# Rotated attention rows stored in reading order, values of four tiles kept in SBUF, query loads ahead of stores

## The chip, the cores and the metric

The kernel runs on one NeuronCore of a Trainium2 chip, in one launch. The time is device microseconds of the whole program. The engines are TensorE (PE, with its weight loads as PEld), VectorE (DVE), ScalarE (ACT), GpSimd (POOL) and SyncE (SP), which here only issues DMAs; 16 DMA engines carry the data. Each engine runs its own list of instructions in order and waits on semaphores.

## The reference

One encoder layer on 2048 tokens of width 1024, fp32. The input is normalised and projected; the columns feed two groups of heads: a sparse attention whose keys an indexer picks, and a gated DeltaNet. Then follow the output projection, an MLP and the last norm.

```python
def sparse_indexer_attention(q, k, v, q_idx, k_idx, w_idx):       # blocks of 128 queries
        rel = jax.nn.relu(jnp.einsum('bqhd,bsd->bqhs', qib, k_idx))
        iscore = jnp.einsum('bqhs,bqh->bqs', rel, wb)             # masked to earlier 64-token chunks
        _, sel = lax.top_k(iscore, topk)                          # 256 keys
        s = jnp.einsum('bqngd,bqknd->bqngk', qg, k_sel) * (A_HEAD_DIM ** -0.5)
        p = jax.nn.softmax(s, axis=-1)
        o = jnp.einsum('bqngk,bqknd->bqngd', p, v_sel)

def reference(x, ...):
        h = rms_norm(x, norm_mix_g)
        (qa, ka, va, qi, ki, wi, qb, kb, vb, zb, bb, ab) = jnp.split(h @ w_in, SPLIT_POINTS, axis=-1)
        qa = rope(qa.reshape(bsz, seq, A_HEADS, A_HEAD_DIM), pos)   # 8 heads of 64
        ka = rope(ka.reshape(bsz, seq, A_KV_HEADS, A_HEAD_DIM), pos)  # 2 heads of 64
        o_a = sparse_indexer_attention(qa, ka, va, qi, ki, wi)
        o_b = gated_deltanet(qb, kb, vb, zb, bb, ab, ...)
        x = x + jnp.concatenate([o_a, o_b], axis=-1) @ w_out
        x = x + jnp.square(jax.nn.relu(rms_norm(x, norm_ffn_g) @ w_ff1)) @ w_ff2
    return rms_norm(x, norm_final_g)
```

Rotating a head of 64 rows needs the head itself and the head with its halves of 32 rows exchanged: x·cos + exchanged(x)·sin.

## The kernel before

All data lies with features on the partitions and tokens on the free axis; a tile is 128 tokens, 16 of them. Matmuls take a high and a low part of each fp32 value, so most operands are split first: ACT rounds the high part, DVE or POOL subtracts it.

There are three stages, each a set of five instruction lists:

1. `norm_and_projection` (0 to about 480 us) normalises the input and projects a part of the columns to `projT` in HBM, one chunk of 128 columns after another.
2. `deltanet_and_selection` (490 to 1463 us) runs the DeltaNet, the indexer's scores and selection, and the projection of the chunks that were left, together. `ROUND` is a hand-written row of 22 slots per round, 18 rounds, 396 slots in all; `ProjectionPlan` and `SelectionPlan` put their steps into these slots. A chain is one chunk times 512 tokens: two halves of matmuls into `p_ps`, evacuation by ACT to `p_out` (`project_out`), and a store by SP (`project_store`). There are 36 chains; 20 of them hold attention queries (chunks C_QA to C_QA+3) or keys (C_KA). For each tile whose scores are wanted, SP loads the indexer's queries in six pieces (`rotated_rows`, lines 496 to 498) and two table rows, POOL rotates them in four steps (`rotation` places load and steps), PE scores, ACT and DVE accumulate. Biases and late scores go to HBM (`biasT`, `scoreT`).
3. `attention_and_mlp` (1463 to 3803 us) runs attention of all 16 tiles in 64 units (four per tile, two heads each) beside output projection and MLP of four token blocks. `OverlapPlan` gives each step a slot; within a slot the list `ORDER` decides. The first 16 units (tiles 0 to 3) run alone, in short slots; then units and dense work (288 loads of weights, `m_raw`, two buffers) share the slots.

What the change and the prediction speak of in stage 3:

- An *item* (`prep_items`) is the k heads (2) or one group of q heads (4) of one tile: 48 in all. `prep_in` loads it as x and exchanged x on 128 partitions, where the two halves of 64 partitions hold the same rows. Items 0 to 11 have five buffers (four in `m_acc`, one in `m_rot`), later ones only `m_rot`; item i waits on `p_done` of the one before in its buffer. DVE multiplies by the cosine (L1992, `by_cosine`), POOL by the sine (L1731), adds (L1738); ACT rounds (L1871); POOL or DVE makes the low part (L1744, L2001). PE's scores (L2122, L2123) need it.
- `table_in` loads the cosine and sine rows of a tile once the tile before has used them (`p_sin`, `p_cos`).
- Values are transposed and split on chip (`m_vsplit`), stored to `valsT` (`values_out`) and read back in pairs of tiles for every unit (`values_back`, `m_vals`, four buffers), 288 loads.
- All of these transfers are issued by SP in its list's order, on one queue.

`rotated_rows` before:

```python
    for base in (0, HD):
        eng.dma_start(a[base:base + HD], src).then_inc(sem_in, 16)
        eng.dma_start(b[base:base + half], src[half:HD]).then_inc(sem_in, 16)
        eng.dma_start(b[base + half:base + HD], src[0:half]).then_inc(sem_in, 16)
```

## Time and profile before

| what | value |
|---|---|
| median of three runs | 3803.68 us (3802.12 to 3806.7) |
| the profiled execution's own time | 3805.14 us |
| its span, first to last instruction | 3803.4 us |
| PE busy | 3389.5 us, 89% |
| DVE, ACT, POOL busy | 55%, 57%, 36% |
| DMA | 306,536 packets, 392.83 MB |
| granted TensorE clock, mean | 0.951 of full speed |

Busy time is time in which an engine executes; issuing a DMA does not count. The profile's 40 slices of 95 us show PE at eight or nine tenths nearly everywhere, with dips at the stages' borders (slices 5, 6 and 16 to 17). A wait is put down to the instruction that released it. Numbers of this profiled execution and of the timed runs differ by 1.5 us.

### The profile page before, as it was taken

The numbers are of one execution on the slowest core, as the hardware profiler recorded it, in microseconds if no ns is written. First come the engines' busy times: TensorE is split into PE (matmuls) and PEld (weight loads), VectorE is DVE, ScalarE is ACT, GpSimd is POOL, SyncE is SP. The second block draws the span as 40 slices with busy tenths as digits, with TensorE's granted clock in tenths as the row PEclk, the third lists the DMA queues.
The fourth block names the chain that finished last, engine by engine and source line by source line (L and its number), as shares of the span: only waits on it lengthen the run. The fifth ranks groups of instructions, "written<-read, shape, count | busy, mean of one in ns | idle before, by whom it ended". The sixth has DMA issues, their size and how long they took to land.

```text
span 3803.4 us, 47244 instructions
## 1 busy us (share of the span) xinstructions
PE 3389.5 (89%) x16866; PEld 2780.1 (73%) x16866; DVE 2073.9 (55%) x3632; ACT 2163.9 (57%) x3717; POOL 1375.3 (36%) x721
## 2 busy tenths in 40 slices
PE   7899967888889994589999889999999999999998
PEld 5678856777777773468777668788777878867886
DVE  4223127787777763636456565757566575433222
ACT  4222127676755552477876859696877944433222
POOL 4111134434254433325344334343323333334442
PEclk9999979999999996699999999999999999999999
DMA  3521151413333243323333333333343333332222
GB/s 115 199 80 70 67 148 50 127 55 80 102 91 86 78 127 104 108 85 112 104 106 117 112 121 107 116 106 123 95 127 120 108 105 101 96 127 84 99 94 78
DMA packets 306536, 392.83 MB, mean 103 GB/s; under 512 B 24688, under 2 KB 231664, under 8 KB 301680
## 3 DMA queue, kind: packets, MB, share of 16 engines
q1 hardware_dynamic: 301552, 358.35, 31.2%
q10 hardware_dynamic: 4752, 31.46, 2.1%
q8 instruction: 136, 2.23, 0.2%
q14 instruction: 96, 0.79, 0.1%
HBM read 323.23 MB, written 66.49 MB: 102 GB/s over the span
## 4 chain that ended last, share of the span: by engine, by line
PE 32%; ACT 13%; DVE 9%; issue 4%; POOL 2%; DMA 1%; SPq 1%; ACTq 0%; DVEq 0%; POOLq 0%
PE m_ps L2059 8%; PE m_ps L2061 8%; PE m_ps L2060 8%; ACT m_junk L1771 5%; PE m_ps L2149 2%; PE m_ps L2137 2%; ACT m_wh L1832 2%; POOL m_wl L1716 1%; ACT m_prob L1859 1%; PE m_ps L2122 1%; ACT m_verdict L1773 1%; PE m_ps L2123 1%; PE m_ps L2102 1%; ACT m_trial L1777 1%; DVE m_rl L1899 1%
## 5 line engine op out<-in xcount | busy, mean ns | idle before, releaser
L1716 POOL TENSOR_TENSOR m_wl<-m_raw,m_wh 128x1024 fp32r<-128x1024 f32 x288 | 717.0, 2490 | 1360.2 <-ACT m_wh L1832 1360.2
L2059 PE MATMUL m_ps<-m_ah,m_wh 128*128 128x512 f32 x1280 | 528.0, 413 | 27.5 <-DVE m_al L1916 16.4
L2061 PE MATMUL m_ps<-m_ah,m_wl 128*128 128x512 f32 x1280 | 506.6, 396 | 0.0
L2060 PE MATMUL m_ps<-m_al,m_wh 128*128 128x512 f32 x1280 | 506.0, 395 | 0.0
L2059 PE MATMUL m_ps<-m_th,m_wh 128*128 128x512 f32 x1024 | 426.4, 416 | 26.0 <-DVE m_tl L1901 11.2
L2061 PE MATMUL m_ps<-m_th,m_wl 128*128 128x512 f32 x1024 | 406.2, 397 | 0.0
L2060 PE MATMUL m_ps<-m_tl,m_wh 128*128 128x512 f32 x1024 | 405.7, 396 | 0.0
L1771 ACT ACTIVATE m_junk<-m_sc,m_trial 128x1152 int8<-128x1152 f32 (+7 forms) x248 | 401.4, 1619 | 4.4 <-DVE m_sc L2019 3.3
L1832 ACT ACTIVATE m_wh<-m_raw 128x1024 fp32r<-128x1024 f32 x288 | 302.8, 1051 | 155.0 <-PE m_ps L2061 139.7
L2059 PEld LDWEIGHTS m_ps<-m_ah,m_wh 128*128 128x128 f32 x1280 | 244.3, 191 | 84.7 <-DVE m_al L1916 19.9
L1177 DVE SCALAR_TENSOR_TENSOR i_score<-i_relu,i_w,i_score 128x512 f32<-128x512 f32 (+3 forms) x266 | 276.5, 1048 | 52.0 <-ACT i_relu L1035 38.6
L1899 DVE TENSOR_TENSOR m_rl<-m_rl 128x512 f32<-128x512 f32 x128 | 106.5, 832 | 361.6 <-ACT m_th L1791 361.2
L1848 ACT ACTIVATE m_phi<-m_ps 128x512 fp32r<-128x512 f32 (+1 forms) x288 | 164.5, 571 | 243.4 <-PE m_ps L2137 238.9
L1894 DVE TENSOR_TENSOR m_acc<-m_acc,m_ps 128x512 f32<-128x512 f32 x256 | 175.0, 685 | 210.0 <-PE m_ps L2061 208.3
L2061 PEld LDWEIGHTS m_ps<-m_ah,m_wl 128*128 128x128 f32 x1280 | 244.2, 191 | 53.7
L1979 DVE TENSOR_TENSOR m_plo<-m_ps,m_phi 128x512 fp32r<-128x512 f32 (+1 forms) x288 | 189.4, 659 | 166.2 <-ACT m_phi L1848 164.9
L2060 PEld LDWEIGHTS m_ps<-m_al,m_wh 128*128 128x128 f32 x1280 | 245.0, 191 | 46.4 <-issue 3.1
L2059 PEld LDWEIGHTS m_ps<-m_th,m_wh 128*128 128x128 f32 x1024 | 196.7, 192 | 72.8 <-DVE m_tl L1901 12.9
L1035 ACT ACTIVATE i_relu<-i_ps 128x512 f32<-128x512 f32 (+3 forms) x304 | 156.2, 545 | 140.8 <-PE i_ps L833 101.4
L1959 DVE CUSTOM_DVE_ANT_0 m_prob<-m_ps,m_bias 128x512 f32<-128x512 f32 (+3 forms) x320 | 192.5, 606 | 73.7 <-PE m_ps L2123 71.5
L2061 PEld LDWEIGHTS m_ps<-m_th,m_wl 128*128 128x128 f32 x1024 | 195.9, 191 | 43.4
L2060 PEld LDWEIGHTS m_ps<-m_tl,m_wh 128*128 128x128 f32 x1024 | 196.8, 192 | 41.1 <-issue 5.0
(313 smaller groups left out, 7510.9 us busy)
## 6 DMA issues: line engine op xcount, KB each, us to landing
m_raw<-w_units SPq DMA_DIRECT2D x288, 512.0 KB, 3.6
m_vals<-valsT SPq DMA_DIRECT2D x256, 128.0 KB, 3.7
p_raw<-w_proj SPq DMA_DIRECT2D x72, 256.0 KB, 4.4
projT<-work ACTq DMA_DIRECT2D x12, 1024.0 KB, 3.8
g_qkvz<-projT SPq DMA_DIRECT2D x16, 768.0 KB, 6.2
wraw<-w_proj SPq DMA_DIRECT2D x21, 512.0 KB, 3.5
projT<-p_out SPq DMA_DIRECT2D x36, 256.0 KB, 3.1
work<-xT SPq DMA_DIRECT2D x8, 1024.0 KB, 5.5
```

The costliest lines, as they stand in the source:

```text
L1035: nc.scalar.activation(relu[:, c % RELUS, 0:w], ips[:, c % 2, 0:w], ACT.Relu).then_inc(relu_done, 1)
L1177: nc.vector.scalar_tensor_tensor(out=to, in0=relu[:, c % RELUS, 0:w], scalar=w_idx[:, j, h:h + 1], in1=to, op0=ALU.mult, op1=ALU.add).then ...
L1716: nc.gpsimd.tensor_tensor(wl[:, n % 3, :], raw[:, n % 2, :], wh[:, n % 3, :].bitcast(fp32), ALU.subtract).then_inc(w_lo, 1)
L1771: turns.do(nc.scalar.activation(junk[:, 0:N], sc[:, 0:N], ACT.Sign, scale=-1.0, bias=trial[:, :].bitcast(fp32), accum_out=balance[:, :]))
L1832: nc.scalar.activation(wh[:, n % 3, :], raw[:, n % 2, :], ACT.Copy).then_inc(w_hi, 1)
L1848: nc.scalar.activation(p_hi[:, m % 2, 0:w], t_bank(r)[:, 0:w], ACT.Copy).then_inc(hi_done, 1)
L1894: nc.vector.tensor_tensor(acc[:, k, :], acc[:, k, :], f_bank(c), ALU.add).then_inc(y_added, 1)
L1959: nc.vector.tensor_tensor_reduce(out=prob[:, u % 2, h, 512 * p:512 * p + w], in0=s_bank(n)[:, 0:w], in1=bias[:, 512 * p:512 * p + w], scal ...
L1979: nc.vector.tensor_tensor(p_lo[:, m % 2, 0:w], t_bank(r)[:, 0:w], p_hi[:, m % 2, 0:w].bitcast(fp32), ALU.subtract).then_inc(lo_done, 1)
L2059: nc.tensor.matmul(dst, hi, rh, start=first, stop=False)
L2060: nc.tensor.matmul(dst, hi, r_low, start=False, stop=False)
L2061: return nc.tensor.matmul(dst, lo, rh, start=False, stop=last)
```

## The change

Five edits, in two stages.

**Layout in HBM.** Two new tensors, `rowsQ` [2 groups, 64 rows, 16 tiles, 2 (x, exchanged x), 4 heads x 128] and `rowsK` [64, 16, 2, 2 heads x 128]. `project_store` writes the 20 chains of queries and keys there, x and exchanged x, with three transfers for each of its two heads, in place of one transfer to `projT`. `p_out` has two buffers, with a semaphore each.

**Loading.** `prep_in` loads an item with one transfer: per row one run of 2 x 4 x 128 (or 2 x 2 x 128) floats, and the 64 rows go to both halves of the partitions by a leading dimension of two with step 0 in the source.

**Values.** `m_vsplit` has five places: tiles 0 to 3 keep theirs, later tiles share the fifth. `product` of tiles 0 to 3 reads them there; `values_back` runs only from tile 4 on, with its buffers counted from unit 16.

**Query loads of the indexer.** `rotation` puts the load first in its slot, ahead of the bias or score store, and the four steps of POOL begin six slots later in place of four.

```diff
     def rotation(self, j, slot):
         slot = max(slot, self.queries_at(j) + 1)
-        self.put("sp", slot, ("load", j))
-        slot += 4
+        self.parts.setdefault(("sp", slot), []).insert(0, ("load", j))
+        slot += 6
...
+        p_stored = [sem(f"p_stored{u}") for u in range(2)]
+        rotated = lambda n: C_QA <= rest.chains[n][1] <= C_KA
+        stores = lambda u, n: 16 * sum(6 if rotated(m) else 1 for m in range(u, n + 1, 2))
...
             def project_store(n):
                 b, c = rest.chains[n]
                 sp.wait_ge(p_left, n + 1)
-                sp.dma_start(projT[c, :, 512 * b:512 * (b + 1)], p_out[:, :]).then_inc(p_stored, 16)
+                if not rotated(n):
+                    sp.dma_start(projT[c, :, 512 * b:512 * (b + 1)], p_out[:, n % 2, :]).then_inc(p_stored[n % 2], 16)
+                    return
+                for h in range(2):
+                    own = p_out[HD * h:HD * (h + 1), n % 2, :].rearrange("p (t s) -> p t s", s=P)
+                    to = rowsK if c == C_KA else rowsQ[(c - C_QA) // 2]
+                    at = (h if c == C_KA else 2 * ((c - C_QA) % 2) + h) * P
+                    own_to = lambda half: to[:, 4 * b:4 * (b + 1), half, at:at + P]
+                    half = HD // 2
+                    sp.dma_start(own_to(0), own).then_inc(p_stored[n % 2], 16)
+                    sp.dma_start(own_to(1)[0:half], own[half:HD]).then_inc(p_stored[n % 2], 16)
+                    sp.dma_start(own_to(1)[half:HD], own[0:half]).then_inc(p_stored[n % 2], 16)
...
             def project_out(n):
                 act.wait_ge(p_done, 2 * (n + 1))
-                if n:
-                    act.wait_ge(p_stored, 16 * n)
+                if n >= 2:
+                    act.wait_ge(p_stored[n % 2], stores(n % 2, n - 2))
...
-                ready = kept[t] if i == self.turns(t) - 1 else self.first
-                self.put("sp", max(ready + 1, product_slot[m - 4] + 1 if m >= 4 else self.first), "values_back", u, i)
+                ready = kept[t] if i == self.turns(t) - 1 else kept[t - 1] if t else self.first
+                if t >= 4:
+                    self.put("sp", max(ready + 1, product_slot[m - 4] + 1), "values_back", u, i)
...
-        v_split = sb("m_vsplit", [P, KV_HEADS, 2 * HD], f32r)
+        v_split = sb("m_vsplit", [P, 5, KV_HEADS, 2 * HD], f32r)
...
             def prep_in(i, before):
-                row, n = (C_KA * P, KV_HEADS) if what == "k" else (C_QA * P + what * G * HD, G)
-                rotated_rows(sp, prep_rows(i, 0), prep_rows(i, 1),
-                             rows[row:row + n * HD, tokens(t)].rearrange("(h r) s -> r h s", r=HD), rot_in[prep_slot(i)])
+                src = (rowsK if what == "k" else rowsQ[what])[:, t].rearrange("r f n -> r (f n)")
+                sp.dma_start(prep_flat(i), src.unsqueeze(0).to_broadcast([2, HD, src.shape[1]])).then_inc(rot_in[prep_slot(i)], 16)
...
             def product(u, i):
-                pe.wait_ge(v_back[m % 4], 16 * (m // 4 + 1))
+                if t < 4:
+                    pe.wait_ge(v_done, t + 1)
+                    v_of = lambda c: v_split[:, c, u % 4 // 2, :]
+                else:
+                    k = back_at(u, i)
+                    pe.wait_ge(v_back[k % 4], 16 * (k // 4 + 1))
+                    v_of = lambda c: vals[:, k % 4, c - 2 * i, :]
...
             def values_back(u, i):
-                if m >= 4:
+                k = back_at(u, i)
+                if k >= 4:
                     sp.wait_ge(pv_done, m - 3)
-                if end == t + 1:
-                    sp.wait_ge(v_kept, 16 * (t + 1))
+                sp.wait_ge(v_kept, 16 * (t + 1 if end == t + 1 else t))
```

How it moves instructions is shown at three places. First SP's list in the opening of stage 3, around the first weights (`m_raw`). Before, the last pieces of item 4 (`m_rot`), the weights, and the pieces of item 5:

```order
L496 DMA m_rot<-projT 64x4x128
L497 DMA m_rot<-projT 32x4x128
L498 DMA m_rot<-projT 32x4x128
L496 DMA m_rot<-projT 64x4x128
L497 DMA m_rot<-projT 32x4x128
L498 DMA m_rot<-projT 32x4x128
L1626 DMA m_raw<-w_units 128x1024 x4
L496 DMA m_acc<-projT 64x4x128
L497 DMA m_acc<-projT 32x4x128
L498 DMA m_acc<-projT 32x4x128
```

After, items 0 to 4 and the weights:

```order
L1662 DMA m_table<-cosT 128x128
L1662 DMA m_table<-sinT 128x128
L1655 DMA m_acc<-rowsK 128x1x512
L1667 DMA m_vraw<-projT 128x128
L1655 DMA m_acc<-rowsQ 128x1x1024 x2
L1655 DMA m_acc<-rowsK 128x1x512
L1655 DMA m_rot<-rowsQ 128x1x1024
L1648 DMA m_raw<-w_units 128x1024 x4
L1655 DMA m_acc<-rowsQ 128x1x1024
```

Six pieces of an item have become one row, so that five rows stand where thirty did, in the same order of items; the line of the issue is 1655 now.

Second, SP's list in stage 2 where the bias of a tile is stored (`biasT`) and the next indexer queries are loaded (`i_rot`). Before:

```order
L678 DMA biasT<-i_ties 128x384
L683 DMA p_raw<-w_proj 128x512
L689 DMA projT<-p_out 128x512
L678 DMA biasT<-i_ties 128x512
L496 DMA i_rot<-projT 64x8x128
L497 DMA i_rot<-projT 32x8x128
L498 DMA i_rot<-projT 32x8x128
```

After:

```order
L702 DMA rowsQ<-p_out 64x4x128
L703 DMA rowsQ<-p_out 32x4x128
L704 DMA rowsQ<-p_out 32x4x128
L702 DMA rowsQ<-p_out 64x4x128
L703 DMA rowsQ<-p_out 32x4x128
L704 DMA rowsQ<-p_out 32x4x128
L682 DMA biasT<-i_ties 128x384
L496 DMA i_rot<-projT 64x8x128
L497 DMA i_rot<-projT 32x8x128
```

The load of the queries now stands between the two bias stores, not behind both, and the store of a chain of queries (`projT<-p_out` before) has become six rows to `rowsQ`.

Third, POOL's list in the second round of stage 2: the first tile's rotation (`i_rot`, `i_qlo`) beside DeltaNet steps (`g_Y`, `g_G`) and low weights (`p_lo`). Before:

```order
L748 TENSOR_TENSOR i_rot<-i_rot,i_table 128x1024
L750 TENSOR_TENSOR i_rot<-i_rot,i_table 128x1024
L753 TENSOR_TENSOR i_rot<-i_rot 128x1024
L787 TENSOR_TENSOR g_Y<-s_ident,g_Ds 128x512
L756 TENSOR_TENSOR i_qlo<-i_rot,i_qhi 128x1024
L801 TENSOR_TENSOR p_lo<-p_raw,p_hi 128x512
```

After:

```order
L764 TENSOR_TENSOR i_rot<-i_rot,i_table 128x1024
L803 TENSOR_TENSOR g_Y<-s_ident,g_Ds 128x512
L766 TENSOR_TENSOR i_rot<-i_rot,i_table 128x1024
L769 TENSOR_TENSOR i_rot<-i_rot 128x1024
L772 TENSOR_TENSOR i_qlo<-i_rot,i_qhi 128x1024
L817 TENSOR_TENSOR p_lo<-p_raw,p_hi 128x512
```

The steps of the rotation begin later, so that `g_Y` of the DeltaNet comes between its first and its second step.

## Rows read from the trace of the kernel before

**Rows 1.** Busy us by stage: window, length, PE, PEld, DVE, ACT, POOL, PEclk, DMA, GB/s
```profile
490.00:1463.00 973.00, 830.77 (x5010) 697.13 (x5010) 691.32 (x1208) 592.94 (x1201) 416.04 (x262) 0.95 0.35 95
1463.00:1611.00 148.00, 58.97 (x273) 47.61 (x274) 70.13 (x223) 53.43 (x137) 52.86 (x49) 0.62 0.41 119
1611.00:3335.00 1724.00, 1620.46 (x7867) 1325.84 (x7866) 1028.09 (x1903) 1252.68 (x2060) 633.84 (x301) 0.97 0.35 109
3335.00:3803.00 468.00, 440.35 (x1863) 351.51 (x1862) 140.42 (x186) 140.14 (x183) 185.71 (x74) 0.97 0.28 96
```

**Rows 2.** PE's waits, 1463 to 1700 us: us in total, times, longest
```profile
PE m_ps L2122 <- POOL m_qlo L1744: 28.1, 2, 26.0
PE m_ps L2158 <- DVE m_mixed L1943: 26.4, 15, 4.4
```

**Rows 3.** PE's waits for DMA, 1620 to 3340 us (the only one)
```profile
PE m_ps L2149 <- DMA m_vals<-valsT: 0.4, 1, 0.4
```

**Rows 4.** Timeline of SP, opening: start, us, engine, line, operation, what, count
```profile
1465.41 0.58 SPq L496 DMA_DIRECT2D m_acc<-projT  x1
...
1482.78 0.43 SPq L498 DMA_DIRECT2D m_rot<-projT  x1
1483.26 9.99 SPq L1626 DMA_DIRECT2D m_raw<-w_units  x4
```

**Rows 5.** Timeline of ACT, POOL and PE, opening; idle time before in brackets
```profile
1487.12 1.06 ACT L1832 ACTIVATE m_wh<-m_raw 128x1024 fp32r<-128x1024 f32 x1 [14.54 <-DMA m_raw<-w_units]
1488.25 4.64 POOL L1716 TENSOR_TENSOR m_wl<-m_raw,m_wh 128x1024 fp32r<-128x1024 f32 x2 [16.13 <-ACT m_wh L1832]
...
1497.50 0.48 PE L2122 MATMUL m_ps<-m_keys,m_qhi 128*128 128x128 f32 x1 [26.00 <-POOL m_qlo L1744]
```

**Rows 6.** Timelines of POOL, then DVE: rows that stand for tables and query rows
```profile
1507.43 0.97 POOL L1731 TENSOR_TENSOR m_acc<-m_acc,m_table 128x256 f32<-128x256 f32 x1 [6.96 <-DMA m_table<-sinT]
...
1526.54 0.97 POOL L1731 TENSOR_TENSOR m_acc<-m_acc,m_table 128x256 f32<-128x256 f32 x1 [6.06 <-DMA m_table<-sinT]
...
1543.85 0.73 POOL L1731 TENSOR_TENSOR m_rot<-m_rot,m_table 128x256 f32<-128x256 f32 x1 [2.63 <-DMA m_table<-sinT]
...
1580.70 0.69 DVE L1992 TENSOR_TENSOR m_rot<-m_rot,m_table 128x512 f32<-128x512 f32 x1 [5.98 <-DMA m_rot<-projT]
...
1595.88 0.68 DVE L1992 TENSOR_TENSOR m_rot<-m_rot,m_table 128x512 f32<-128x512 f32 x1
```

**Rows 7.** DMA, 3400 to 3700 us: packets; queue with MB, share; issues, KB, landing
```profile
DMA packets 7645, 27.98 MB, mean 93 GB/s; under 512 B 848, under 2 KB 848, under 8 KB 7632
...
q1 hardware_dynamic: 7632, 27.79, 27.2%
...
m_raw<-w_units SPq DMA_DIRECT2D x53, 512.0 KB, 3.4
```

**Rows 8.** Window of the first stage with the highest DMA share; columns as in rows 1
```profile
120.00:140.00 20.00, 12.37 (x46) 10.09 (x47) 1.69 (x1) 6.17 (x6) 7.07 (x3) 0.74 0.95 358
```

**Rows 9.** DMA issues, whole span: KB each, median us from issue to landing
```profile
m_raw<-w_units SPq DMA_DIRECT2D x288, 512.0 KB, 3.6
...
m_rot<-projT SPq DMA_DIRECT2D x126, 64.0 KB, 2.9
...
m_table<-cosT SPq DMA_DIRECT2D x16, 64.0 KB, 2.0
```

**Rows 10.** Timelines of SP and ACT: one weights load and its split
```profile
2503.91 0.35 SPq L1626 DMA_DIRECT2D m_raw<-w_units  x1
...
2516.55 1.05 ACT L1832 ACTIVATE m_wh<-m_raw 128x1024 fp32r<-128x1024 f32 x1
```

**Rows 11.** SP's longest wait, 490 to 1463 us
```profile
SPq L689 <- ACT p_out L1111: 348.6, 32, 31.4
```

**Rows 12.** Waits of POOL and of PE, 490 to 1463 us
```profile
POOL i_rot L748 <- DMA i_table<-sinT: 63.8, 8, 15.7
...
PE p_ps L963 <- POOL p_lo L801: 16.6, 5, 4.0
```

More of the change, by code:

```diff
@@ L521, in deltanet_and_selection @@
         q_hi, q_lo = sb("i_qhi", [P, 2, IDX_HEADS, P], f32r), sb("i_qlo", [P, 2, IDX_HEADS, P], f32r)
-        p_out = sb("p_out", [P, 512])
+        p_out = sb("p_out", [P, 2, 512])
         ones = sb("g_ones", [P, P])
@@ L583, in deltanet_and_selection @@
         w_in = [sem(f"p_w_in{u}") for u in range(rest.RAW)]
-        p_high, p_low, p_done, p_left, p_stored = map(sem, " p_high p_low p_done p_left p_stored".split())
+        p_high, p_low, p_done, p_left = map(sem, " p_high p_low p_done p_left".split())
+        p_stored = [sem(f"p_stored{u}") for u in range(2)]
+        rotated = lambda n: C_QA <= rest.chains[n][1] <= C_KA
+        stores = lambda u, n: 16 * sum(6 if rotated(m) else 1 for m in range(u, n + 1, 2))
         dve_s, act_s, pool_s, pe_s = sem("g_dve"), sem("g_act"), sem("g_pool"), sem("g_pe")
@@ L662, in selection @@
                         if stored_chains:
-                            sp.wait_ge(p_stored, 16 * (max(stored_chains) + 1))
+                            for u in range(2):
+                                sp.wait_ge(p_stored[u], stores(u, max(stored_chains)))
                         rotated_rows(sp, rot[:, 0], rot[:, 1], rows[C_QI * P:C_QI * P + IDX_HEADS * HD, tokens(j)]
@@ L727, in _ @@
                 sp.wait_ge(kept[u], 16 * len([z for z in plan.late_piece.values() if z % 4 == u]))
-            sp.wait_ge(p_stored, 16 * len(rest.chains))
+            for u in range(2):
+                sp.wait_ge(p_stored[u], stores(u, len(rest.chains) - 1))
         @block.gpsimd
@@ L1105, in project_out @@
                 act.wait_ge(p_done, 2 * (n + 1))
-                if n:
-                    act.wait_ge(p_stored, 16 * n)
-                else:
+                if n >= 2:
+                    act.wait_ge(p_stored[n % 2], stores(n % 2, n - 2))
+                elif n == 0:
                     for u in range(2):
                         act.wait_ge(z_stored[u], 16 * ((N_PROJECTED + 1 - u) // 2))
-                nc.scalar.activation(p_out[:, :], pps[:, :], ACT.Copy).then_inc(p_left, 1)
+                nc.scalar.activation(p_out[:, n % 2, :], pps[:, :], ACT.Copy).then_inc(p_left, 1)
             run_turns(selection, ("act", {"high": project_high, "evac": project_out, "block": project_block}), front, back)
@@ L1611, in attention_and_mlp, with prep_flat @@
         heads_of = lambda i: 2 if plan.prep_items[i][1] == "k" else 4
+        def prep_flat(i):
+            r = acc[:, 2 * prep_slot(i):2 * prep_slot(i) + 2, :] if prep_slot(i) < 4 else rot[:, :, :]
+            return r.rearrange("p f n -> p (f n)")[:, 0:2 * heads_of(i) * P]
         def prep_rows(i, half):
-            r = acc[:, 2 * prep_slot(i):2 * prep_slot(i) + 2, :] if prep_slot(i) < 4 else rot[:, :, :]
-            return r[:, half, 0:heads_of(i) * P].rearrange("p (h s) -> p h s", s=P)
+            return prep_flat(i)[:, half * heads_of(i) * P:(half + 1) * heads_of(i) * P].rearrange("p (h s) -> p h s", s=P)
+        v_own = lambda t: v_split[:, min(t, 4), :, :]
+        back_at = lambda u, i: plan.turn[u, i] - plan.turn[16, 0]
         last_turn = lambda u: plan.turn[u, plan.turns(u // 4) - 1]
@@ L1654, in values_back @@
                 end = min(2 * i + 2, t + 1)
-                if m >= 4:
+                k = back_at(u, i)
+                if k >= 4:
                     sp.wait_ge(pv_done, m - 3)
-                if end == t + 1:
-                    sp.wait_ge(v_kept, 16 * (t + 1))
-                sp.dma_start(vals[:, m % 4, 0:end - 2 * i, :].bitcast(fp32),
-                             valsT[2 * i:end, :, g * P:(g + 1) * P].rearrange("c p d -> p c d")).then_inc(v_back[m % 4], 16)
+                sp.wait_ge(v_kept, 16 * (t + 1 if end == t + 1 else t))
+                sp.dma_start(vals[:, k % 4, 0:end - 2 * i, :].bitcast(fp32),
+                             valsT[2 * i:end, :, g * P:(g + 1) * P].rearrange("c p d -> p c d")).then_inc(v_back[k % 4], 16)
             def score_load(n):
@@ L1836, in values_hi @@
                 act.wait_ge(ring_done, r + 1)
-                if t:
+                if t > 4:
                     act.wait_ge(v_kept, 16 * t)
-                nc.scalar.activation(v_split[:, :, 0:HD], t_bank(r)[:, 0:P].rearrange("p (g d) -> p g d", d=HD),
+                nc.scalar.activation(v_own(t)[:, :, 0:HD], t_bank(r)[:, 0:P].rearrange("p (g d) -> p g d", d=HD),
                                      ACT.Copy).then_inc(v_high, 1)
@@ L2148, in product @@
                         at = 2 * P * (c - 2 * i)
-                        last = nc.tensor.matmul(o, vals[:, m % 4, c - 2 * i, :], part[:, m % 2, at:at + 2 * P],
+                        last = nc.tensor.matmul(o, v_of(c), part[:, m % 2, at:at + 2 * P],
                                                 start=(c == 0 and part is p_hi), stop=(c == t and part is p_lo))
@@ L2164, in _, with program @@
                     does[what](*x)
-def program(nc, S, a, projT, biasT, scoreT, valsT, mixT, xhT, xlT, outT):
+def program(nc, S, a, projT, rowsQ, rowsK, biasT, scoreT, valsT, mixT, xhT, xlT, outT):
     topk = min(TOPK_MAX, S // 4)
@@ L2252 @@
     xhT, xlT = [nc.dram_tensor(n, (S // 512, P, KC, 512), fp32, kind="Internal").ap() for n in ("xhT", "xlT")]
+    rowsQ = nc.dram_tensor("rowsQ", (2, HD, S // P, 2, 4 * P), fp32, kind="Internal").ap()
+    rowsK = nc.dram_tensor("rowsK", (HD, S // P, 2, KV_HEADS * P), fp32, kind="Internal").ap()
     mixT = nc.dram_tensor("mixT", (KC, P, S), fp32, kind="Internal").ap()
     outT = nc.dram_tensor(_OUT, (KC, P, S), fp32, kind="ExternalOutput").ap()
-    program(nc, S, a, projT, biasT, scoreT, valsT, mixT, xhT, xlT, outT)
+    program(nc, S, a, projT, rowsQ, rowsK, biasT, scoreT, valsT, mixT, xhT, xlT, outT)
     r = run_bass_kernel_spmd(nc, [arrays], core_ids=[0])
```

18 lines of the change are left out of this document (9 added, 9 removed).

## The prediction

> **What bounds the kernel now.** I read the busy times by stage first. TensorE (PE) is busy for 94% of the long stretch from 1611 to 3335 us and for 94% of the last one, and 85% of the time from 490 to 1463; in the 148 us from 1463 to 1611 it is busy for 59 us [rows 1]. So time is bought by PE work everywhere but in that gap, the opening of the attention stage, where only query and key rows are rotated and the first 16 small units run. The granted clock there is 0.62 in the mean, so it stands much of the time at the lower of its two levels (1.2 GHz), against 0.95 to 0.97 elsewhere; PE has little to do before and in it. PE's waits in 1463 to 1700 come next: 28.1 us for the low part of the queries (one wait of 26.0) and 26.4 on DVE's normalising [rows 2]. In 1620 to 3340 PE waits for a transfer for 0.4 us in all [rows 3]: nothing that the change does to DMA can buy time there, it can only cost.
>
> **The opening as it is.** SP issues two table loads and then five items (k and two q of tile 0, k and q of tile 1) as 30 pieces, 1465.41 to 1483.21, before it reaches the weights [rows 4]. The weights land at 1487.1, ACT and POOL split two units, POOL rotates, and PE's first score is at 1497.50 [rows 5]. After that the next tile's cosine table is late behind other issues: POOL stands 7.0 us until 1507.4, 6.1 until 1526.5 and 2.6 until 1543.9, DVE with it at the first two, and DVE 6.0 until 1580.7 for the q rows of tile 4 [rows 6].
>
> **What the edit takes away there.** An item is one issue: 30 issues become 5 at 0.43 to 0.58 us, which saves about 15 us in front of the weights. In the first four tiles the 24 reads of values go, and SP waits less for `pv_done`. Were every load to land as quickly as loads do now, this is worth: first score 13 us earlier (15 of issue, less 2 because 2.5 MB at 358 GB/s [rows 8] then take 7 us with the weights at their end); the table of tile 1 needs only `p_sin` and `p_cos`, so 5.5 of the 7.0 us go; 4 of the 6.1 at the second (beyond that DVE has other work); 5 of the 6.0 at 1580.7; 2.9 at the mix loads, where six pieces sit between the third and fourth [rows 4, 6]. Sum 13 + 5.5 + 4 + 5 + 2.9 = 30.4 us.
>
> **What the new load costs: the deciding term.** No row of the trace shows a load like the new one. Its source access is [2 copies, step 0] x [64 rows] x [run], its destination 128 rows. All loads and stores before have 16, 32, 64 or 128 rows outermost on both sides. How work is dealt to the 16 DMA engines can be read where weights run alone: 53 loads of 512 KB make 7,632 packets, 144 each, and 848 of them are small, 16 for each load [rows 7]. That is 128 rows of 4 KB, eight to each engine, and a closing packet on each of 16. So a transfer is dealt out by its outermost rows. The new one has two outermost. Dealt as now, it lands as the weights do, in 3.6 us [rows 9]; dealt in two, each engine gets 64 rows. The trace gives 27.79 MB in 27.2% of 16 x 300 us, 21.3 GB/s per engine [rows 7], and 358 GB/s at a share of 0.95, 23.6 GB/s [rows 8]: 256 KB per engine takes 11.1 to 12.3 us for a q item, half as much for a k item, plus about 2 us to land (the small table loads: 2.0 us [rows 9]). The bounds of this term are thus 3.6 and 14.3 us per q item. The nearest row by size is the lower; by shape there is none, and I take the upper, because the dealing that rows 7 show leaves no other place to cut. The chances below carry the doubt.
>
> The Trainium skill ("DMA: Bandwidth & Descriptors", Rules for kernel authors) says it outright: a leading zero-stride broadcast of c copies confines the whole DMA to at most c engines. No run here shows it yet; by that rule the time is the slow one.
>
> **The walk through the opening, two engines.** All loads are on SP's one queue, so whatever follows has its share on those two engines behind them. With 12.3 and 6.1 us (in brackets with 11.1 and 5.6):
> 1. Ahead of the weights stand 3 q and 2 k items: 49 us (44.5). The weights' own share is 1.5, landing 2: 1465.4 + 49 + 1.5 + 2 = 1518, against 1487.1: +31 (+26). The splits, rotation and first score follow as in [rows 5]: PE starts at 1528 in place of 1497.5.
> 2. The next q and k items are issued after the fourth weights load and at the first score; table 1 stands behind both and lands at 1546.7, where the shifted row would want 1538.5: +8.2 (+6.4).
> 3. Three items (q, q, k) are freed only by the rows after table 1 and stand ahead of table 2: +16.3 (+13.3).
> 4. Two q items stand ahead of table 3, where there was slack of 2.6 us on POOL alone: +11.8 (+9.4).
> 5. The q items of tile 4: the first behind 2 MB of x, +6.5 (+4.6); the second, which DVE wants at 1595.9 [rows 6] and which is issued when the first is done, +6.8 (+5.6); a k item ahead of the fourth mix load: +2.4 (+1.5).
> Sum 83 (67); I take the middle, **+75 us**. The 30 us of savings are not subtracted: SP's issues are no longer what ends any of these waits, the landings are. The clock is not a term of its own; the late start keeps PE at the lower level for longer in a stretch that waits on data anyway.
>
> **The long stretch.** Eleven more tiles load two q and a k item each, 20 us or more apart, and cos and sin wait for them far less soon. But weights land behind them. A weights load is used late: issued at 2503.91, split by ACT at 2516.55 [rows 10], so 12.6 less 3.6 leaves 9 us of cover. A q item issued up to 7.6 us earlier (the spacing of weights: 1724 us over some 225 units) delays it by 4.7 to 12.3 us: in some half of 22 cases ACT stands 0 to 3 us. PE takes over a part: +6 us, between 0 and 25. The values' reads have about three turns of lead and go with it.
>
> **The middle stage (490 to 1463).** 20 of 36 stores of the projection become six pieces: 5 x 0.53 us more each, 53 us of SP's time. SP waits 348.6 us there just for ACT to leave a chain, so the weights behind it have cover [rows 11]; without it each store would cost 2.7 us. The query loads now stand ahead of the bias and score stores, and their rotation is two slots later. POOL stood 63.8 us for these loads, PE 16.6 us for the low weights that POOL makes behind them [rows 12]: a gain of up to 12. Against it, scores start two slots later and end at slot 385 in place of 381 of 396: some 5 scores of 0.8 us PE move to the end, and order shifts of up to 10 us either way. I take -3 (-12 to +10). The double `p_out` frees 2.7 us of ACT at most.
>
> Sum: 75 + 6 - 3 = +78 on the span of 3803.4, 3881. The profiled run itself took 3805.1, 1.5 over the median of 3803.7; on the median the forecast is **3882 us**, with 3840 to 3920 as its own range (67 - 12 - 15 for packets somewhat quicker; 83 + 25 + 10).
>
> **Rivals.**
> - *Loads are dealt to 16 engines* (faster). The price is then 3.6 us in place of 14.3 and the opening gains 30.4 us; with 3 from the middle stage 3770. It decides if a q item lands in less than about 5 us. For it: the 126 pieces of 64 KB land 2.9 us after issue in the median [rows 9], the bytes are the same and the runs are longer. Against: these have no copy dimension.
> - *Two engines, but other transfers do not queue behind* (slower, less). Then the weights are early and the first score waits for q alone: 1465.4 + 6.1 + 12.3 + 2, and 4.6 of rotation and rounding give 1490. Only the items' own stream of 31 us for each tile binds: the last q of tile 3 lands near 1591 where it is wanted at 1556, +33, and tile 4's add 12: 3850.
> - *The price is hidden or offset* (no change): it takes twelve items in 110 us; two engines need 100 to 112 us for them before any gap, so hiding needs loads that never wait for a free slot, and they do (`p_done`).
> - *The edit does not do what it says*: rows would be read in the wrong order or six pieces remain; the order of the program shows one.
>
> **Chances.** Two engines with the queue behind them 0.62; the same with free lanes 0.14; sixteen engines 0.18; the rest 0.06. A measurement of this kernel tells 0.2% (7.6 us) from no change. Faster 0.17, same 0.05, slower 0.78. The range that leaves out less than 2 in 10 must reach to the fast rival: 3766 to 3925.
>
> **What would show it.** For the two-engine price: q items that land 12 us or more after issue with a DMA share of about 0.13 while SP sits in waits; the first weights near 1518, first score near 1528 (if the middle stage ends at the same time); stands of POOL and DVE put down to the sine table and to `m_rot`, of 16 and 12 us; an opening of some 220 us in place of 148. Against it: q items at 4 us, weights at about 1474 and the first score at 1484. The stores' price shows as SP's waits for `p_left` shrinking by about 50 us with no new wait of ACT on the projection's weights; the long stretch's as ACT waits on `m_raw`. If PE's busy time in the long stretch falls under 92%, the +6 was too small. I am wrong if the first score comes earlier than 1497.

## The result, and the profile after

The changed kernel takes 3875.99 us (median; 3869.3 to 3881.1), the kernel before on the same chip 3802.9: ratio 1.0188, 95% interval 1.0175 to 1.0201. It is slower, 6 us under the forecast of 3882. The profiled execution's span is 3870.8 us, 67.4 more than before.

Three instants divide it. They are read from PE's timeline: the last matmul of the middle stage (L848 before, L864 after), the first score, and the first dense matmul.

| profile | middle stage ends | first score | first dense matmul | span | timed ratio |
|---|---|---|---|---|---|
| before | 1456.6 | 1497.5 | 1611.4 | 3803.4 | |
| after | 1440.2 | 1506.2 | 1666.7 | 3870.8 | 1.0188 |
| difference of the stretch | -16.4 | +25.1 | +46.6 | +12.1 | |

So the opening costs 71.8 us more, the rest of the stage 12.1, and the middle stage gives 16.4. By stage, as in [rows 1], with the borders where this kernel has them (window, length, busy us of PE, PEld, DVE, ACT, POOL, then PEclk, DMA share, GB/s):

```profile
490.00:1441.00 951.00, 818.95 (x5010) 693.78 (x5010) 683.58 (x1208) 590.49 (x1199) 412.30 (x261) 0.96 0.40 101
1441.00:1667.00 226.00, 62.11 (x277) 50.80 (x277) 71.44 (x225) 55.60 (x140) 54.50 (x50) 0.58 0.21 69
1667.00:3391.00 1724.00, 1608.96 (x7811) 1315.71 (x7811) 1025.92 (x1897) 1247.08 (x2049) 631.54 (x299) 0.97 0.35 108
```

PE does the same work in the opening (62 us) in 226 us, and the DMA engines, at a share of 0.21, are less busy there than the 0.41 of [rows 1]. In the next 1724 us PE is busy 11.5 us less than before: that is the +12.

SP's timeline of the opening, which answers to [rows 4] (start, us, line, what):

```profile
1448.96 0.62 SPq L1655 DMA_DIRECT2D m_acc<-rowsK  x1
...
1450.10 4.18 SPq L1655 DMA_DIRECT2D m_acc<-rowsQ  x2
1454.32 9.94 SPq L1655 DMA_DIRECT2D m_acc<-rowsK  x1
1464.30 9.97 SPq L1655 DMA_DIRECT2D m_rot<-rowsQ  x1
```

The instructions that wait for these items, on DVE, ACT and PE (as in [rows 5]; idle time before in brackets):

```profile
1457.50 1.00 DVE L2013 TENSOR_TENSOR m_acc<-m_acc,m_table 128x256 f32<-128x256 f32 x1 [16.40 <-DMA m_acc<-rowsK]
1467.78 0.69 DVE L2013 TENSOR_TENSOR m_acc<-m_acc,m_table 128x512 f32<-128x512 f32 x1 [9.29 <-DMA m_acc<-rowsQ]
...
1495.81 1.06 ACT L1853 ACTIVATE m_wh<-m_raw 128x1024 fp32r<-128x1024 f32 x1 [35.99 <-DMA m_raw<-w_units]
...
1506.20 0.47 PE L2143 MATMUL m_ps<-m_keys,m_qhi 128*128 128x128 f32 x1 [48.01 <-POOL m_qlo L1765]
```

The q item, 512 KB, lands 10.3 us after the k item ahead of it. From 1467.8, a q, a k and a q item more (10.3 + 5.1 + 10.3, k taken as half) and some 2 us for the weights make 1495.5: they are there at 1495.81. The window in which only items run shows how many engines carry them:

```profile
1455.00:1475.00 20.00, 0.45 (x1) 0.18 (x1) 2.11 (x3) 0.42 (x1) 1.45 (x2) 0.50 0.13 51
```

A share of 0.13 of 16 is two engines, with 51 GB/s. Of PE's clock this row says that it stands at the lower level (0.50, 1.2 GHz), where PE had been idle for the 16.6 us before 1457.7. The stands of POOL (its idle time in front of an instruction) that answer to [rows 6], first three for tables, then for the q rows of tile 4:

```profile
1521.94 0.97 POOL L1752 TENSOR_TENSOR m_acc<-m_acc,m_table 128x256 f32<-128x256 f32 x1 [12.77 <-DMA m_table<-sinT]
...
1554.34 0.97 POOL L1752 TENSOR_TENSOR m_acc<-m_acc,m_table 128x256 f32<-128x256 f32 x1 [19.37 <-DMA m_table<-sinT]
...
1581.32 0.73 POOL L1752 TENSOR_TENSOR m_rot<-m_rot,m_table 128x256 f32<-128x256 f32 x1 [12.30 <-DMA m_table<-sinT]
...
1626.60 1.77 POOL L1752 TENSOR_TENSOR m_rot<-m_rot,m_table 128x512 f32<-128x512 f32 x1 [18.53 <-DMA m_rot<-rowsQ]
```

Two views of waits, for the rest. First 490 to 1463 us (as in [rows 11, 12]), then all after 1667 us (as in [rows 3]):

```profile
SPq L702 <- ACT p_out L1127: 192.7, 19, 20.5
...
SPq L694 <- ACT p_out L1127: 118.4, 14, 17.1
...
POOL i_rot L764 <- DMA i_table<-sinT: 17.0, 6, 5.8
...
PE p_ps L979 <- POOL p_lo L817: 4.1, 2, 2.8
```

```profile
PE m_ps L2176 <- DMA m_vals<-valsT: 9.4, 5, 4.3
ACT m_wh L1853 <- DMA m_raw<-w_units: 7.7, 4, 3.6
```

### The profile page after: what moved, and what is told of

Same layout as the page of the kernel before. It is cut to its first block, busy times and chain, and to the rows that moved or that the text cites. A ratio compares the mean times of both kernels' runs of the same rounds, so it can differ in the third digit from the quotient of the medians.

```text
span 3870.8 us, 47278 instructions
## 1 busy us (share of the span) xinstructions
PE 3382.9 (87%) x16866; PEld 2781.4 (72%) x16866; DVE 2064.7 (53%) x3632; ACT 2163.1 (56%) x3717; POOL 1373.5 (35%) x721
## 3 DMA queue, kind: packets, MB, share of 16 engines
q1 hardware_dynamic: 276240, 360.96, 31.2%
## 4 chain that ended last, share of the span: by engine, by line
PE 30%; ACT 12%; DVE 8%; DMA 4%; issue 4%; POOL 2%; SPq 1%; ACTq 0%; DVEq 0%; POOLq 0%
PE m_ps L2080 8%; PE m_ps L2082 8%; PE m_ps L2081 8%; ACT m_junk L1792 5%; PE m_ps L2176 2%; PE m_ps L2158 2%; ACT m_wh L1853 2%; POOL m_wl L1737 1%; ACT m_prob L1880 1%; PE m_ps L2143 1%; PE m_ps L2144 1%; ACT m_verdict L1794 1%; ACT m_trial L1798 1%; PE m_ps L2123 1%; DMA out_dram<-m_tmp 1%
## 5 line engine op out<-in xcount | busy, mean ns | idle before, releaser
L2080 PE MATMUL m_ps<-m_ah,m_wh 128*128 128x512 f32 x1280 | 529.1, 413 | 27.5 <-DVE m_al L1937 16.6
L1193 DVE SCALAR_TENSOR_TENSOR i_score<-i_relu,i_w,i_score 128x512 f32<-128x512 f32 (+3 forms) x266 | 252.7, 957 | 49.5 <-ACT i_relu L1051 35.0
L1051 ACT ACTIVATE i_relu<-i_ps 128x512 f32<-128x512 f32 (+3 forms) x304 | 156.0, 546 | 166.9 <-PE i_ps L849 132.3
```

The source lines that it names most:

```text
L1051: nc.scalar.activation(relu[:, c % RELUS, 0:w], ips[:, c % 2, 0:w], ACT.Relu).then_inc(relu_done, 1)
L1193: nc.vector.scalar_tensor_tensor(out=to, in0=relu[:, c % RELUS, 0:w], scalar=w_idx[:, j, h:h + 1], in1=to, op0=ALU.mult, op1=ALU.add).then ...
L2080: nc.tensor.matmul(dst, hi, rh, start=first, stop=False)
```

## The experiments

My theory, A: the transfer is dealt to the DMA engines by its outermost dimension, here of two entries, and everything behind it on the queue waits. Rivals: the new layout in HBM, or the copying itself, is slow. A second question is what the other edits are worth. All ratios below are against the kernel before on the same chip.

**e1: an item in two transfers.**

```diff
-                sp.dma_start(prep_flat(i), src.unsqueeze(0).to_broadcast([2, HD, src.shape[1]])).then_inc(rot_in[prep_slot(i)], 16)
+                for base in (0, HD):
+                    sp.dma_start(prep_flat(i)[base:base + HD], src).then_inc(rot_in[prep_slot(i)], 16)
```

> The changed kernel, but an item is loaded by two transfers, one for each half of 64 partitions, so that 64 rows are outermost in each; everything else stays. Theory A (a transfer is dealt to the DMA engines by its outermost dimension, and two outermost entries are what costs): an item lands in about 4 us, the weights about 15 us after the first item's issue plus 7, first score some 27 us after the middle stage's end instead of 66. The opening's +72 goes and the 30.4 us worked out for the saved issues come; with the 16.5 us that the middle stage gained in the profile of the changed kernel: 3803.4 - 16.5 - 30.4 = 3757, between 3750 and 3775. Theory B (the cost lies in the new layout in HBM or in its reads, whoever carries them): no change, 3876 as the changed kernel, over 3850.

Measured: 3765.4 us, ratio 0.9898 (0.9884 to 0.9913), span 3762.9. It is faster than both kernels. SP, ACT and PE, and a window with items only:

```profile
1449.84 1.14 SPq L1656 DMA_DIRECT2D m_acc<-rowsK  x2
...
1456.60 12.73 SPq L1648 DMA_DIRECT2D m_raw<-w_units  x4
```
```profile
1463.20 1.06 ACT L1854 ACTIVATE m_wh<-m_raw 128x1024 fp32r<-128x1024 f32 x1 [7.56 <-DMA m_raw<-w_units]
...
1473.60 0.48 PE L2144 MATMUL m_ps<-m_keys,m_qhi 128*128 128x128 f32 x1 [19.55 <-POOL m_qlo L1766]
```
```profile
1452.00:1460.00 8.00, 0.45 (x1) 0.18 (x1) 2.11 (x3) 0.42 (x1) 1.45 (x2) 0.50 0.96 239
```

The same bytes from the same place, with 64 rows outermost: the share goes from 0.13 to 0.96, and 110 us of the kernel's time go with it. Layout and stores are the same, so theory B falls. The first score is 32.6 us after the middle stage's end, 8.3 nearer than in the kernel before, but later than the 27 expected. The items' ten issues take 6.8 us (1449.84 to 1456.60) where thirty took 17.9, 11.1 less and not 15; and the first weights are there 6.6 us after their issue, behind the items, where it was 3.9 [rows 4, 5]. (The expectation of e9 below puts this first score at 1474.8: that is the fifth score matmul.) The opening (end of the middle stage to first dense matmul) is 132.3 us, against 154.8 before and 226.6 after; the rest of the stage, 2189.5, has lost its +12.

**e2 and e5: no copy.** The lower half of the partitions gets other rows, by a step of the source that is not 0; which heads or tokens these are is wrong, nothing else changes. e2 takes the other group of query heads (for k the neighbouring tile), e5 the neighbouring tile for both:

```diff
-                src = (rowsK if what == "k" else rowsQ[what])[:, t].rearrange("r f n -> r (f n)")
+                src = (rowsK if what == "k" else rowsQ[what])[:, t // 2 * 2:t // 2 * 2 + 2].rearrange("r a f n -> a r (f n)")
```

> The changed kernel with one transfer for an item, two outermost entries as there, but the second entry is other data (the other group of query heads, or the neighbouring tile's keys) instead of the same rows again, so the lower half of the partitions gets wrong rows. Theory A (it is the two outermost entries): time as the changed kernel, 3876 within 8; a q item every 10.3 us. Theory B (it is the copy, that is step 0 or reading the same addresses twice): the time falls to about 3757 as with 16 engines.

> As e2_two_sources, whose q items read rows 0 to 127 of one block at a constant distance, so that two and 64 could be joined to 128 rows. Here the second entry is always the neighbouring tile (4 KB or 2 KB away, while the rows are 64 or 32 KB apart), for q and for k, so that two entries stay outermost; half of the rows are of the wrong tile. Nothing is copied. Theory A (two outermost entries that can't be joined with the rows): as the changed kernel, 3876 within 8, q items 10 us apart, DMA share 0.13 while they run. Theory B (a copy with step 0, or reading the same addresses twice, is what costs): about 3765, as e1_two_loads.

e2 gave 3787.9 us, 0.9957 (0.9942 to 0.9971), which fits neither theory as I had written them. The fault was in the design: group 1 of `rowsQ` begins just where row 64 of group 0 would stand, so the q items' access is 128 rows at one distance, not two times 64. Its trace bears this out: two q items are issued in 0.91 us, the seven in `m_acc` land in 6.9 us in the median, and in the 3 us in which the first two run all 16 engines are busy.

```profile
1448.25 0.91 SPq L1658 DMA_DIRECT2D m_acc<-rowsQ  x2
```
```profile
m_acc<-rowsQ SPq DMA_DIRECT2D x7, 512.0 KB, 6.9
```
```profile
1450.00:1453.00 3.00, 0.00 (x0) 0.00 (x0) 0.00 (x0) 0.00 (x0) 0.00 (x0) 0.50 1.00 301
```

Only the k items keep two outermost entries there. e5 closes that gap: 3871.5 us, 1.0182 (1.0164 to 1.0200), the changed kernel's ratio. SP again needs 10 us for an issue, and the share in a window with items only is 0.13:

```profile
1444.26 3.96 SPq L1655 DMA_DIRECT2D m_acc<-rowsQ  x2
1448.27 9.91 SPq L1655 DMA_DIRECT2D m_acc<-rowsK  x1
1458.22 9.97 SPq L1655 DMA_DIRECT2D m_rot<-rowsQ  x1
```
```profile
1450.00:1470.00 20.00, 0.44 (x1) 0.18 (x1) 2.11 (x3) 0.42 (x1) 1.45 (x2) 0.50 0.13 52
```

So it is not the copy: two outermost entries cost the same with step 0 and with other data, and where they join with the rows (the q items of e2) the transfer keeps all 16 engines. The Trainium skill ("DMA: Bandwidth & Descriptors", Rules for kernel authors) names the broadcast as an example of a small outermost dimension; e5 shows the general rule without one, and the trace agrees.

**e3: four entries outermost** (the first 32 rows four times, so the others are wrong).

```diff
-                ... src.unsqueeze(0).to_broadcast([2, HD, src.shape[1]])
+                ... src[0:32].unsqueeze(0).to_broadcast([4, 32, src.shape[1]])
```

> The changed kernel with one transfer for an item, four outermost entries: the first 32 rows copied four times, so the rows 32 to 63 of each half are wrong. Bytes and destination are the same. Theory A: four engines, an item in half the time (5.2 us for q, 2.6 for k in place of 10.3 and 5.1). Ahead of the first weights then stand 20.6 us in place of 41.2, so the first score comes about 20 us earlier; the tables' stands (5.8, 13.3 and 9.7 us later than before) shrink to at most 2 us together, since an item pair of 7.7 us fits behind the tile's work. About 3757 + 14 for the slower start + 2 = 3773, between 3762 and 3800. Theory B (copies as such cost): no faster than 3870.

3815.4 us, 1.0033 (1.0022 to 1.0044), between e1 and the changed kernel. In a window with items only the share is 0.25 of 16, four engines:

```profile
1455.00:1462.00 7.00, 0.45 (x1) 0.18 (x1) 1.00 (x1) 0.17 (x1) 1.45 (x2) 0.50 0.25 81
```

The first score is 17.6 us nearer to the stage's end than in the changed kernel (48.4 against 66.0; about 20 expected). But the forecast of 3773 was 42 us too low. POOL's waits for tables and rows do not vanish:

```profile
1502.42 0.97 POOL L1752 TENSOR_TENSOR m_acc<-m_acc,m_table 128x256 f32<-128x256 f32 x1 [6.46 <-DMA m_table<-sinT]
...
1523.55 0.97 POOL L1752 TENSOR_TENSOR m_acc<-m_acc,m_table 128x256 f32<-128x256 f32 x1 [8.09 <-DMA m_table<-sinT]
...
1583.55 1.77 POOL L1752 TENSOR_TENSOR m_rot<-m_rot,m_table 128x512 f32<-128x512 f32 x1 [14.98 <-DMA m_rot<-rowsQ]
```

Here DVE starts on q 6.9 us after k (1459.92 and 1466.81), not 5.2: four engines carry 81 GB/s, 20 each, where two carry 51, 25 each. With 16 engines, too, the items of e1 move 239 GB/s in place of the 358 of [rows 8]. The opening is 173.3 us, 41 over e1's, the rest of the stage 10.5 over e1's, for which I had allowed nothing.

**e4, e11, e12: the move of the indexer's query loads, alone on the kernel before**, whole, and by halves: the load first in its slot (e11), or POOL's steps six slots later in place of four (e12).

```diff
-        self.put("sp", slot, ("load", j))
-        slot += 4
+        self.parts.setdefault(("sp", slot), []).insert(0, ("load", j))
+        slot += 6
```

> The kernel before with only the move of the indexer's query loads: the load first in its slot, the four steps of POOL six slots later in place of four. Opening, layout, values and p_out as before. Theory A (the move is what made the middle stage 16.5 us shorter): 3803 - 14 = 3789, between 3785 and 3793. Theory B (the second buffer of p_out did it, since SP's stores no longer hold ACT): within 4 us of 3803. My forecast on record had -3 for the move, between -12 and +10.

> The kernel before, with only the order inside the slot changed: the indexer's query load ahead of the bias or score store; POOL's steps stay four slots later. With the move as a whole at 0.9974 (e4). Theory A (the store that waits for DVE holds the load, so order is what matters): 0.998, and POOL's wait for the table falls from 63.8 us to under 40. Theory B (the load is merely late for four slots, whatever stands ahead): 1.000 and POOL's wait over 50.

> The kernel before, with only the distance changed: POOL's four steps six slots after the load in place of four, the load still behind the stores. Theory A (order is what matters): within 0.1% of 1.000, POOL's wait for the table over 40 us. Theory B (distance is what matters): 0.9975, and the wait falls from 63.8 us to about 20, as in e4.

| | ratio | 95% interval | middle stage ends |
|---|---|---|---|
| e4, both | 0.9974 | 0.9963 to 0.9985 | 1444.2 |
| e11, load first | 0.9983 | 0.9974 to 0.9991 | 1447.4 |
| e12, six slots | 0.9979 | 0.9970 to 0.9987 | 1446.9 |

POOL's waits for the table in 490 to 1463 us, of e4, e11 and e12; 63.8 before:

```profile
POOL i_rot L748 <- DMA i_table<-sinT: 18.9, 6, 6.0
```
```profile
POOL i_rot L748 <- DMA i_table<-sinT: 40.7, 5, 16.9
```
```profile
POOL i_rot L748 <- DMA i_table<-sinT: 48.6, 10, 12.2
```

The move is worth 10 us, nearer to theory A of e4 than to B, and either half a part of it: 23 and 15 us of POOL's wait, which with both come to 45. Neither of the two theories for e11 and e12 holds by itself. PE's own wait on POOL's low weights, 16.6 us before, is 4.3 in e4, 9.4 in e11 and 4.2 in e12; by this the distance alone does for PE what both do. But the intervals of the three ratios overlap, so how the 10 us divide stays open.

**e6 and e7: layout and values.** e6 is the changed kernel with stores to `projT` and six pieces for an item; e7 is e1 with the values of all tiles read back.

```diff
-                if not rotated(n):
-                    sp.dma_start(projT[c, :, 512 * b:512 * (b + 1)], p_out[:, n % 2, :]).then_inc(p_stored[n % 2], 16)
-                    return
...
+                sp.dma_start(projT[c, :, 512 * b:512 * (b + 1)], p_out[:, n % 2, :]).then_inc(p_stored[n % 2], 16)
...
+                rotated_rows(sp, prep_rows(i, 0), prep_rows(i, 1),
+                             rows[row:row + n * HD, tokens(t)].rearrange("(h r) s -> r h s", r=HD), rot_in[prep_slot(i)])
```
```diff
-                if t >= 4:
-                    self.put("sp", max(ready + 1, product_slot[m - 4] + 1), "values_back", u, i)
+                self.put("sp", max(ready + 1, product_slot[m - 4] + 1 if m >= 4 else self.first), "values_back", u, i)
```

> The changed kernel with its layout in HBM undone: queries and keys go to projT in one store for each chain, and an item is loaded in six pieces from there, as in the kernel before; values in SBUF, the second buffer of p_out and the moved query loads stay. Theory A (the layout, loaded by 16 engines, is worth what e1_two_loads has over this): opening as before but for the values, 3804 - 10 (the move, as measured in e4) - 5 (24 reads less, each 0.4 us of SP's issues and its wait) = 3789, so that the layout's own part in e1's 3765 is 24. Theory B (the gain of e1_two_loads comes from the values and the middle stage): within 5 us of 3765.

> e1_two_loads (an item in two transfers) with the values of tiles 0 to 3 stored and read back for each unit as in the kernel before. Theory A (24 reads and their waits stand in front of the loads on SP's queue in the opening): +3 to +8 over e1_two_loads' 3765, seen between the first score and the first dense matmul. Theory B (SP has room in the opening once items are two issues): within 2 us.

e6: 3786.0 us, 0.9954 (0.9941 to 0.9967). e1 is 0.0056 lower: the layout, loaded by 16 engines, is worth some 21 us, 24 expected. In the two profiles 15.4 of them are in the opening, 4.6 in where the middle stage ended, which one profile can't tell (see e8). The opening of e6 is 147.7 us, 7.1 less than before, and all of that after the first score. e7: 3775.8, 0.9925 (0.9910 to 0.9940), 10 over e1, of which the opening shows 6.4 (138.7 against 132.3); the intervals just overlap, and the rest is where the middle stage ended (1445.6 against 1441.0), which this edit does not touch. The values' part is thus 6 to 7 us in the opening by two pairs of profiles.

**e8: p_out used as one buffer** (on e1).

```diff
-                if n >= 2:
-                    act.wait_ge(p_stored[n % 2], stores(n % 2, n - 2))
-                elif n == 0:
+                if n:
+                    act.wait_ge(p_stored[(n - 1) % 2], stores((n - 1) % 2, n - 1))
+                else:
```

> e1_two_loads with p_out used as if it had one buffer: ACT waits for the stores of the chain just before, six for a chain of queries or keys. Theory A (the double buffer pays for the six stores): about 20 chains times up to 2.5 us that ACT waits longer, of which PE takes over a part, and the middle stage, 15.8 us shorter in the mean of four profiles that have both edits against 12.4 with the move alone, gets longer by 3 to 12 us. Theory B (ACT's waits there are covered): within 3 us.

3772.4 us, 0.9917 (0.9903 to 0.9931); e1 has 0.9898 with an interval up to 0.9913, so this is not settled. The middle stage ends at 1445.7. Eight profiles with the changed kernel's middle stage, word for word the same program there, end it between 1434.3 and 1445.6 (mean 1441.3): one profile can't tell 4 us. What the trace has is small: ACT stands 1.9 us in all for a store, and PE 6.7 us for ACT's evacuation:

```profile
ACT p_out L1127 <- DMA projT<-p_out: 1.9, 1, 1.9
```
```profile
PE p_ps L979 <- ACT p_out L1127: 6.7, 4, 5.0
```

**e9 and e10: the first weights behind the first tiles**, on e1 and on the changed kernel. This asks what the +31 of my walk's first step is worth by itself.

```diff
-            self.put("sp", self.first + 2 if n < 2 else self.first + 3 if n < 4 else self.unit_slot[n - 4] + 1, "weights", n)
-            s = self.unit_slot[n - 2] if n >= 2 else self.first + 5
+            self.put("sp", self.first + 20 if n < 2 else self.first + 32 if n < 4 else self.unit_slot[n - 4] + 1, "weights", n)
+            s = self.unit_slot[n - 2] if n >= 2 else self.first + 30
```

> e1_two_loads with the first dense weights put behind the first tiles: two units of weights are loaded 18 slots later and split 25 slots later, the next two loaded 29 slots later, so that neither SP's queue nor POOL's list has them in front of the first query item's rotation. Theory A (in the opening, the first score waits for POOL, which waits for the weights; the query rows had landed at 1456 and the score came at 1474.8): the first score about 11 us earlier; POOL's 4.6 us of splits come back inside the opening. 3765 - 11 + 2 = 3756, between 3750 and 3761, faster than both kernels. Theory B (the opening is one chain through the tables and items, and an earlier start is spent on the next wait): within 3 us of 3765.

> The changed kernel (an item in one transfer, two engines) with the first weights put behind the first tiles in the same way. It asks how much of the opening's +72 is weights that stand behind items on the queue. Theory A (what counts is that stream of items itself, 25.7 us for each tile on two engines, and the queue behind it): the first score comes about 30 us earlier, but the later tiles' rows are then waited for instead, as in my second rival; 3876 - 26 = 3850, between 3838 and 3865. Theory B (the delayed start is a cost of its own that nothing takes over): the whole 33 us between the landing of q at 1467.8 plus 5 of rotation and the first score at 1506.2 come back: 3843 or less.

e10: 3872.6 us, 1.0186 (1.0172 to 1.0199), nothing gained. PE's first score and the three table stands of POOL:

```profile
1475.15 0.47 PE L2143 MATMUL m_ps<-m_keys,m_qhi 128*128 128x128 f32 x1 [14.87 <-POOL m_qlo L1765]
```
```profile
1512.79 0.97 POOL L1752 TENSOR_TENSOR m_acc<-m_acc,m_table 128x256 f32<-128x256 f32 x1 [28.88 <-DMA m_table<-sinT]
...
1549.11 0.97 POOL L1752 TENSOR_TENSOR m_acc<-m_acc,m_table 128x256 f32<-128x256 f32 x1 [23.29 <-DMA m_table<-sinT]
...
1580.35 0.73 POOL L1752 TENSOR_TENSOR m_rot<-m_rot,m_table 128x256 f32<-128x256 f32 x1 [12.70 <-DMA m_table<-sinT]
```

The first score comes 33.0 us after the middle stage's end in place of 66.0, and the 33 us are lost again at the next three stands (12.8 to 28.9, 19.4 to 23.3, 12.3 to 12.7) and in the work between. The first dense matmul is at 223.8 us from the stage's end in place of 226.6. What ends the opening is the chain of items on two engines, tables and rotations, wherever the weights stand. Of that chain the stream of items is only a part: SP also stands until a rotation frees an item's buffer (`p_done`), in e10 for 49 us between 1448 and 1660:

```profile
SPq L1655 <- POOL m_qlo L1765: 25.1, 3, 10.4
...
SPq L1655 <- DVE m_keys L2022: 23.9, 4, 18.0
```

On e1 the same edit brings the first score 11.9 us nearer to the stage's end (20.7 against 32.6), 6.7 us of it remain at the first dense matmul (125.7 against 132.3) and 3.2 at the end, and the time is 3765.7, 0.9904 (0.9891 to 0.9917): no difference from e1. Theory B of e9 holds. Of e10 neither does: A named the mechanism but forecast 26 us of gain; the medians differ by 3, which the intervals don't tell from none.

## Why the prediction was right

**The deciding choice**, two engines rather than 16, rested on the packets of [rows 7] and held: the share is 0.13, and e1 (0.96), e5 (0.13) and e3 (0.25) tie it to the outermost dimension. My price per q item (12.3 us) was too slow, even the bracketed one (11.1): 10.3 us was measured, 25.5 GB/s per engine. With two engines at work each is quicker than the 21 to 24 GB/s that I had read where all 16 run.

**The walk.** Differences between before and after, each instant taken from the one ahead of it:

| step | forecast (with quicker packets) | measured |
|---|---|---|
| middle stage | -3 | -16.4 |
| 1, first weights, first score | +31 (+26) | +25.1 |
| 2, table 1 | +8.2 (+6.4) | +5.8 |
| 3, table 2 | +16.3 (+13.3) | +13.3 |
| 4, table 3 | +11.8 (+9.4) | +9.7 |
| 5, tile 4 and mix loads | +15.7 (+11.7) | +17.9 |
| opening | +75 (67 to 83) | +71.8 |
| rest of the stage | +6 (0 to 25) | +12.1 |
| sum | +78 | +67.4 |

The steps 1 to 4 came as the bracketed values say, since the items were that quick. Step 5 came larger: by DVE's rows the first q rows of tile 4 cost 8.4 us more, the second 5.6, and what follows until the first dense matmul 3.9, for 6.5, 6.8 and 2.4 ([rows 6] and these):

```profile
1626.55 0.69 DVE L2013 TENSOR_TENSOR m_rot<-m_rot,m_table 128x512 f32<-128x512 f32 x1 [10.08 <-DMA m_rot<-rowsQ]
...
1647.29 0.69 DVE L2013 TENSOR_TENSOR m_rot<-m_rot,m_table 128x512 f32<-128x512 f32 x1 [5.36 <-DMA m_rot<-rowsQ]
```

As an account of causes step 1 is misread, though: e10 shows that the late first score costs nothing of its own. The sum was right because each step was counted from the one ahead in the order that the kernel has. My rival with free lanes reasoned from the items' stream alone and put the end at 3850; the weights, 46.9 us after the first item's issue, and the late tables show that transfers do queue behind the items, and with the weights moved away (e10) the end is still 3872.6. The rival counted on 31 us for each tile throughout. In e10 the stands for the tables are 36.3 and 31.2 us apart though three items need 25.7: the stream also stops between items, and SP's waits for `p_done` above fill the gaps at least in part. Two of the prediction's sums are off without changing the forecast: from 1556 to 1591 are 35 us, not 33, and twelve items take two engines 111 to 123 us at its own prices, not 100 to 112 (103 at the measured ones).

That the time came within 6 us of the forecast is in part luck: in the profiles the opening is 3 us and the middle stage 13 us under their terms, the rest of the stage 6 over.

**The middle stage** is the term that was mis-sized, and in the profile outside my bounds (-12 to +10). The gain of up to 12 us that I named came nearly whole: POOL's wait for the table fell from 63.8 to 17.0, and PE's wait on POOL from 16.6 to 4.1. What failed is the 9 us that I set against it for later scores and a shifted order: timed alone (e4) the move is worth 10 us. The profile overstates that, so about 6 of the 16.4 are the scatter between executions or the second buffer of `p_out`, which e8 could not price. The five stores more for each of 20 chains cost nothing that can be seen: SP's waits for the evacuation went from 348.6 to 311.1, 38 us where I had 50, and ACT has no wait for a store.

**The rest of the stage**: I named ACT's waits for weights (+6). There are 7.7 us of them, but PE's own for the values' reads, 9.4, stand beside; I had dismissed these as three turns ahead. In e1 the waits of PE and ACT on both are gone or under 0.5 us, and so is the +12.

**The fast rival** (16 engines, 3770 by my sum) is what e1 makes: 3765.4. Its opening gained 22.5 us where I had 30.4: the first score 8.3 for 13 (ten issues in place of five, and weights that land later behind the items), table 1 5.5 for 5.5, table 2 4.8 for 4, and the q rows of tile 4 with the mix loads 4.0 for 7.9. The middle stage's 15.6 in place of 3 makes up for it.

## What to carry to other kernels

Before replacing many transfers by one, look at the outermost dimension of the one: a pair of halves or a copy put outermost confines it to as many engines as it has entries, and one transfer for each entry, with the rows outermost, keeps all of them. On a shared queue, charge that price to everything that stands behind, tables and weights too. And where a stream of transfers sets the pace, moving one thing out of its way moves the wait, not the end: count the stream, with the waits for the buffers that it fills, and not the first wait.

## What the runs showed that I had not expected

- **The issue itself can stand.** I had expected SP in waits, with issues of 0.5 us. Instead, an issue takes 9.94 and 9.97 us in the changed kernel (0.62 for the first), about as long as a q item takes: SP is held by the transfers ahead, as I read it, where it waits for no semaphore.
- **A DMA engine is quicker with few at work.** Two engines carry 51 GB/s (25 each), four 81 in e3 (20 each), sixteen 239 on the items of e1 (15 each) at a share of 0.96, while weights reach 358 at 0.95 [rows 8]. Rows here stand 64 KB apart in HBM (32 KB for keys) and each is read twice (in e3 four times). The q items of e2 have the same distance but are not read twice, and ran at 301 GB/s for 3 us; they also fill 128 partitions with one transfer, so which of these makes the items of e1 slower is not shown.
- **The same program scatters in its middle stage** by 11 us between profiles of different kernels that share it (1434.3 to 1445.6), while 23 timed runs of the kernel before lie between 3796.6 and 3809.5. A stage's gain under that size needs timed runs.
